# Rotary partner rows moved by transfers, and sample index products in quarter arrays, in a two-layer hybrid decoder step

## The reference

```python
h = rms_norm(x, norm_g) * (1 + scale) + shift
zq, zk, zv, zqi, zki, zwi, ... = split_in(h @ w_in)
q  = rope(rms_norm(zq,  q_norm_g), pos)       # 8 heads of 128
k  = rope(rms_norm(zk,  k_norm_g), pos)       # 2 heads of 128
qi = rope(zqi, pos)                           # 16 index heads of 64
ki = rope(rms_norm(zki, idx_k_norm_g), pos)   # 1 index key of 64

def rope(x, pos):      # rd = width // 4, half = rd // 2
    out = concat([x1 * cos - x2 * sin, x2 * cos + x1 * sin, x[rd:]])

dots  = einsum('bthd,bsd->bths', qi, ki) * 64 ** -0.5
score = einsum('bths,bth->bts', relu(dots), wi)     # then the top k, then attention
```

## Time and profile before

| what | value |
|---|---|
| median of three executions | 3576.96 us |
| the profiled execution: its time, its span | 3580.12 us, 3578.3 us |
| PE busy (matmuls) | 3489.2 us, 98% of the span |
| PEld, DVE, POOL, ACT busy | 3230.0, 1745.4, 1215.5, 1061.9 us |
| granted TensorE clock, mean | 0.99 |
| time of the DMA queue's packets | 53.8% of 16 engines' span |

### The profile page before, as it was taken

How to read it: one execution, slowest core, us unless ns; L and a number is a source line. 1 busy time by engine, 2 the same in 40 slices (tenths; PEclk the granted TensorE clock), 3 DMA queues, 4 the chain that set the end, 5 groups by cost and what they waited for, 6 DMA issues and landing times. The chain is left out here.

```text
span 3578.3 us, 66830 instructions
## 1 busy us (share of the span) xinstructions
PE 3489.2 (98%) x27774; PEld 3230.0 (90%) x27774; DVE 1745.4 (49%) x2484; ACT 1061.9 (30%) x1500; POOL 1215.5 (34%) x508
## 2 busy tenths in 40 slices
PE   5899999999999999999998999999999999999999
PEld 3699988989989989998888999888899998899999
DVE  1413578968987113321115145789689851233201
ACT  2322222222552333222223222222235423332221
POOL 0233333435424223333323333234263232234433
PEclk9799999999999999999999999999999999999999
DMA  9733333656544774658885555444332257644442
GB/s 323 258 104 103 97 104 99 182 171 180 173 126 137 251 229 164 214 192 286 284 283 161 163 156 169 134 127 108 89 111 90 74 174 235 214 157 131 129 122 94
DMA packets 557130, 590.48 MB, mean 165 GB/s; under 512 B 73564, under 2 KB 523377, under 8 KB 546747
## 3 DMA queue, kind: packets, MB, share of 16 engines
q1 hardware_dynamic: 556828, 586.21, 53.8%
HBM read 546.37 MB, written 116.39 MB: 185 GB/s over the span
## 5 line engine op out<-in xcount | busy, mean ns | idle before, releaser
L804 POOL TENSOR_TENSOR w_lo_t<-raw,w_hi_t 128x1024 fp32r<-128x1024 f32 x472 | 1170.5, 2480 | 2339.5 <-ACT w_hi_t L817 2339.5
L1115 PE MATMUL acc<-act_hi,w_hi_t 128*128 128x272 f32 x6528 | 1403.7, 296 | 35.1 <-DVE u_s L1619 14.3
L1115 PE MATMUL acc<-act_hi,w_lo_t 128*128 128x272 f32 x6528 | 1354.0, 289 | 0.0
L1115 PE MATMUL acc<-act_lo,w_hi_t 128*128 128x272 f32 x6528 | 1350.6, 288 | 0.0
L1115 PEld LDWEIGHTS acc<-act_hi,w_hi_t 128*128 128x128 f32 x6528 | 1030.2, 189 | 121.0 <-issue 86.3
L1115 PEld LDWEIGHTS acc<-act_lo,w_hi_t 128*128 128x128 f32 x6528 | 1028.9, 189 | 0.0
L1115 PEld LDWEIGHTS acc<-act_hi,w_lo_t 128*128 128x128 f32 x6528 | 1024.0, 190 | 0.0
L817 ACT ACTIVATE w_hi_t<-raw 128x1024 fp32r<-128x1024 f32 x472 | 499.9, 1059 | 1638.5 <-PE acc L1115 1622.5
L1657 DVE SCALAR_TENSOR_TENSOR conv<-conv,cw 128x512 f32<-128x512 f32 x240 | 197.9, 825 | 70.1 <-POOL w_lo_t L804 70.1
L1115 PE MATMUL acc<-m_hi,w_hi_t 128*128 128x272 f32 x1024 | 215.8, 292 | 0.0
L1115 PE MATMUL acc<-m_hi,w_lo_t 128*128 128x272 f32 x1024 | 211.5, 288 | 0.0
(11 more groups left out here) (242 smaller groups left out, 2714.2 us busy)
## 6 DMA issues: line engine op xcount, KB each, us to landing
raw<-in_w_in_dram SPq DMA_DIRECT2D x272, 512.0 KB, 3.7
ada_ring<-in_w_ada_dram SPq DMA_DIRECT2D x95, 512.0 KB, 7.2
raw<-in_w_in_dram SPq DMA_DIRECT2D x136, 256.0 KB, 3.3
k_near<-in_cache_k_dram SPq DMA_DIRECT2D x256, 128.0 KB, 2.8
v_near<-in_cache_v_dram SPq DMA_DIRECT2D x256, 128.0 KB, 2.7
k_ring<-k_near SPq DMA_DIRECT2D x64, 512.0 KB, 5.1
v_page<-v_near SPq DMA_DIRECT2D x64, 512.0 KB, 6.5
raw<-in_w_out_dram SPq DMA_DIRECT2D x64, 512.0 KB, 4.2
```

What stands on the lines that cost most here:

```text
L804: pool.tensor_tensor(w_lo_t[:, m % 2], raw[:, m % 4], w_hi_t[:, m % 2].bitcast(F32), ALU.subtract).then_inc(S.w_lo, 1)
L1115: last = pe.matmul(acc[:, 2 * m + h, 0:HALF], w[:, c % 2, k, P * m:P * m + P], r[:, kt, h * HALF:(h + 1) * HALF], start=first and k == 0 a ...
```

## The change

1. `tile_extras` no longer makes the exchanged rows. SP, in its `aside`, waits until ACT has evicted the tile and copies the partner rows from `stage[:, m]` to `stage[:, 6 + m]` by transfers within SBUF (`swap_rows`): four of 8 rows x 544 columns for tiles of index heads, two of 16 rows for K and Q. DVE clears `stage[:, 6:8]` once a layer, behind `layer_input`, since the other rows have to be zero. `rope` waits for the transfers (`swap_in`), multiplies the tile by the cosine and the exchanged rows by the sine, both in SBUF, and goes on as before. Index query tiles have no PE work left behind their halves.
2. `dots_s` runs once per sequence: four products of 64 x 64 x 512 (rows 64 p, output partitions 64 c with c = (f + p) mod 2), bank p of `aux`. One relu of 2 x 512 columns follows, and one mixing piece of four products of 64 x 32 x 512 in step 3. `qi_blk` has 64 columns and is not cleared any more. The wait for `conv_s_done` moves from the first product to `dots_tail`, and `turn_kx` waits for the relu of the sequence before.
3. Some semaphores are merged or renamed (`q_blocked`, `blanks_set`, `v_taken`), with the numbers that are waited for.

```diff
+def swaps(g):
+    if g == N_V:
+        return []
+    if g < N_K:
+        return [(a + 8 * s, a + 8 - 8 * s, 8) for a in (0, ID) for s in range(2)]
+    return [(16 * s, 16 - 16 * s, 16) for s in range(2)]
...
+            def swap_rows(l, g, m):
+                if g == N_KI and m == 1 or g == N_V:
+                    return
+                sp.wait_ge(acc_free[m], acc_set(l, g) + 1)
+                if g == N_KI or g == N_QI and m == 1:
+                    sp.wait_ge(S.blanks_set, 3 + l)
+                for to, at_, rows_ in swaps(g):
+                    sp.dma_start(stage[to:to + rows_, 6 + m, :], stage[at_:at_ + rows_, m, :]).then_inc(swap_in[m], 16)
...
                 if l > 0 and 1 <= n < 17:
                     gather([(x, kv) for x in staged_at(n, i)], S.kv_staged)
+                if 1 <= n <= N_GLU and i < 2:
+                    swap_rows(l, n - 1, i)
...
-                    elif s <= 2:
-                        f = 17 * l + 2 * b + s
-                        act.wait_ge(S.sdots_ready, f)
-                        if 2 * b + s > 2:
-                            act.wait_ge(S.mixed, f - 2)
-                        act.activation(relu_s[:, s - 1, :], aux[:, 2, :], ACT.Relu).then_inc(S.srelu_done, 1)
+                    elif s == 1:
+                        act.wait_ge(S.sdots_ready, 9 * l + b + 1)
+                        if b >= 1:
+                            act.wait_ge(S.mixed, 9 * l + b)
+                        act.activation(relu_s[:, :, :], aux[:, 0:2, :], ACT.Relu).then_inc(S.srelu_done, 1)
...
-                    if g == N_KI or g >= N_K:
-                        j = 0 if g == N_KI else 1 + m if g == N_K else 3 + 2 * (g - N_Q) + m
-                        need(pe, S.std_ready, 11 * l + j)
-                        fp32_pair(0, con[:, T_ONE64:T_ONE64 + P] if g == N_KI else ones, stage[:, 2 + m, :])
-                    sw = T_SWI if g < N_K else T_SWQ
-                    last = fp32_pair(2, con[:, sw:sw + P], stage[:, m, :])
+                    j = 0 if g == N_KI else 1 + m if g == N_K else 3 + 2 * (g - N_Q) + m
+                    need(pe, S.std_ready, 11 * l + j)
+                    last = fp32_pair(0, con[:, T_ONE64:T_ONE64 + P] if g == N_KI else ones, stage[:, 2 + m, :])
...
-                need(pe, S.kx_copied, 8 * l + b)
+                need(pe, S.srelu_done, 9 * l + b)
...
-                pe.matmul(aux[:, 2, :], qi_blk[:, b, :], kx_t[:, f, :], start=True, stop=True).then_inc(S.sdots_ready, 1)
+                for f in range(2):
+                    for p in range(2):
+                        c = (f + p) % 2
+                        last = pe.matmul(aux[64 * c:64 * c + 64, p, :], qi_blk[64 * p:64 * p + 64, b, :], kx_t[64 * p:64 * p + 64, f, :],
+                                         start=True, stop=True)
+                last.then_inc(S.sdots_ready, 1)
...
-                for p in range(2):
-                    j = 2 * f + p
-                    last = pe.matmul(aux[32 * j:32 * j + 32, 3, :], mixw[:, p, b, :], relu_s[:, f, :], start=b == 0, stop=b == SEQS - 1)
+                for f in range(2):
+                    for p in range(2):
+                        c, j = (f + p) % 2, 2 * f + p
+                        last = pe.matmul(aux[32 * j:32 * j + 32, 3, :], mixw[64 * c:64 * c + 64, c, b, :], relu_s[64 * c:64 * c + 64, p, :],
+                                         start=b == 0, stop=b == SEQS - 1)
...
-                    if 1 <= s <= 2:
-                        dots_s(l, b, s - 1)
-                    if s >= 2:
-                        mix_s(l, b, s - 2)
+                    if s == 1:
+                        dots_s(l, b)
+                    if s == 3:
+                        mix_s(l, b)
...
-                dve.tensor_tensor(pair(swapped), aux[:, 2:4, 0:HALF], pair(cs[:, sin, :]), ALU.mult).then_inc(S.swap_used, 1)
+                dve.wait_ge(swap_in[m], swap_landed(l, g, m))
                 st.then(dve.tensor_tensor(x, x, cs[:, cos, :], ALU.mult))
+                st.then(dve.tensor_tensor(swapped, swapped, cs[:, sin, :], ALU.mult))
```

More of the change, by code:

```diff
@@ L284, in values_at, with swap_landed @@
     return logits_at(b) + 3
+def swaps(g):
[4 more added lines that the diff above has]
+    return [(16 * s, 16 - 16 * s, 16) for s in range(2)]
+def swap_landed(l, g, m):
+    tiles = [x for x in range(N_GLU) if not (x == N_KI and m == 1)]
+    return 16 * sum(len(swaps(x)) * (l + (x <= g)) for x in tiles)
 def staged_at(n, i):
@@ L372, in trunk_kernel @@
         relu_p = at(C + 7808, "relu_p", [P, 2, 512])
-        qi_blk = at(C + 9408, "qi_blk", [P, SEQS, P])
+        qi_blk = at(C + 9408, "qi_blk", [P, SEQS, 64])
         kx = at(C + 11072, "kx", [P, 2, 2, 4, 2, ID])
@@ L1156, in tile_extras @@
             def tile_extras(l, g, m):
-                if g == N_KI and m == 1:
+                if g == N_KI and m == 1 or N_QI <= g < N_K:
                     return
-                r = 0 if g == N_KI else 2 * g - 1 + m
                 if g == N_KI and l == 1:
@@ L1247, in mix_s @@
                 last.then_inc(S.mixed, 1)
             def dots_tail(l):
-                pe.wait_ge(S.srelu_done, 17 * l + 16)
+                pe.wait_ge(S.srelu_done, 9 * l + 8)
+                pe.wait_ge(S.conv_s_done, 8 * l + 8)
                 for b in range(SEQS):
-                    last = pe.matmul(aux[0:64, 2, STEPS * b:STEPS * b + STEPS], qi_blk[0:64, b, 0:64],
+                    last = pe.matmul(aux[0:64, 2, STEPS * b:STEPS * b + STEPS], qi_blk[0:64, b, :],
                                      ki_new[0:64, SEQ + STEPS * b:SEQ + STEPS * b + STEPS], start=True, stop=True)
@@ L1551, in rope @@
                 r = 0 if g == N_KI else 2 * g - 1 + m
[L1552 removed]
                 if g == N_V:
+                    dve.wait_ge(S.aux_ready, 13 * l + 4 + m)
                     dve.tensor_copy(v_tok[:, 0:4, m * HD:(m + 1) * HD], aux[:, 2, :].rearrange("p (t d) -> p t d", t=4)).then_inc(S.rope_done, 1)
[L1555 removed]
+                    dve.tensor_copy(v_tok[0:NS, 4, m * HD:(m + 1) * HD], aux[0:NS, 3, 0:P]).then_inc(S.v_taken, 1)
                     return
@@ L1572, in rope @@
                     st.wait()
-                    dve.tensor_tensor(out, swapped, std, ALU.mult).then_inc(S.rope_done, 1)
+                    dve.tensor_tensor(out, x, std, ALU.mult).then_inc(S.rope_done, 1)
                 else:
-                    dve.tensor_tensor(out, swapped, x, ALU.add).then_inc(S.rope_done, 1)
+                    dve.tensor_tensor(out, x, swapped, ALU.add).then_inc(S.rope_done, 1)
             def tok(l):
@@ L1663, in turn_qi @@
                 dve.wait_ge(S.tok_stored, 96 * (l + 1))
-                st.then(dve.memset(qi_blk[:, :, :], 0.0))
-                st.wait()
                 dve.wait_ge(S.rope_done, 21 * l + 21)
@@ L1669, in turn_qi @@
                         src = qi[64 * h:64 * h + 64, :, SEQ:TOK].rearrange("p j (b t) -> p b j t", t=STEPS)
-                        c0 = 64 * p + 32 * h
-                        last = dve.tensor_copy(qi_blk[64 * p:64 * p + 64, :, c0:c0 + 32].rearrange("p b (j t) -> p b j t", t=STEPS), src)
-                last.then_inc(S.diag_done, 1)
+                        last = dve.tensor_copy(qi_blk[64 * p:64 * p + 64, :, 32 * h:32 * h + 32].rearrange("p b (j t) -> p b j t", t=STEPS), src)
+                last.then_inc(S.q_blocked, 1)
             def as_bias(work, scores):
@@ L1742, in turn_q @@
                     last = dve.tensor_copy(q_blk[:, :, g, 16 * g:16 * g + 16].rearrange("p b (j t) -> p b j t", t=STEPS), src)
-                last.then_inc(S.qblk_done, 1)
+                last.then_inc(S.q_blocked, 1)
             def keep_k(l, b, j):
@@ L2028, in _ @@
                 layer_input(l)
+                dve.memset(stage[:, 6:8, :], 0.0).then_inc(S.blanks_set, 1)
                 for n in range(NG):
```

51 lines of the change are left out of this document (23 added, 28 removed).

## The result

The kernel after takes 3520.42 us (median of four executions, 3518.45 to 3521.8) against 3578.5 us for the kernel before on the same chip (3575.09 to 3582.82). The ratio is 0.9838, with a 95% interval of 0.9822 to 0.9853. The profiled execution has a span of 3519.5 us, 58.8 us under the one before. The forecast was 3517.0 us: 60.0 us less than before, where the medians now differ by 58.1 and the spans by 58.8.

The account below looks back on a forecast made before the run. PE was taken as the bound between its waits at the places touched. 34.8 + 26.2 - 1.0 = 60.0 us off the median 3576.96 gave 3517.0 us, with 3509 to 3536 for 8 in 10.

Parts of the forecast that it names:

- Exchange products removed: Rotary tiles: 38 tiles each lose exchange products costing 0.915 us, taking 34.8 us off PE.
- Index products: Samples' index products: a sequence's pieces fall from 4.08 to 2.44 us (dots 1.26, mixing 1.18), 26.2 us over 16.
- What waits in the index stage: Index stage: DVE's 35.1 us of waiting for POOL cover rounds that shrink by 0.82 us, so nothing is charged.
- New transfers: Partner-row transfers: tight only at the last rotary tile, 0.3 us left there; charged 0.5 us a layer, 1.0 us.
- three signs that I had named for being wrong: PE's idle time growing over 3 us, a four-product piece over 1.6 us, or transfers landing later than 5 us.
- Rival A: Mixing products of two row groups take turns at bank 3 of `aux`: 3544.5 us, or 3530.8 with two turns; chance 0.13.
- B: Transfers land late, so `rope` holds the key transposes or ACT's eviction, and PE: 3522 us at 6 us landings; chance 0.10.
- C: Index stage's quarter products run one after another, 7.60 us a sequence, and the kernel gets slower: 3599.5 us; chance 0.02.
- D: ACT and POOL set the rotary stage's pace, so the 34.8 us return as waits for `w_lo`: 3551 us; chance 0.02.

Follow-up runs that it names:

- swaps_later: The change with the transfers of the partner rows issued one chunk (6.0 us) later for every tile; span 3540.5 us.
- two_quarters: The change with the four dots products put into two quarters of the array, leaving out half of the samples' scores; span 3529.3 us.
- gate_later: The change with DVE's wait for POOL in the convolution steps put one chunk later in the index stage; 3520.38 us (0.9843).
- after_again: The changed kernel run once more, unedited; 3521.57 us, span 3519.8 us.
- index_only: The kernel before with item 2 of the change only (quarter products, one relu, one mixing piece a sequence); 3552.31 us (0.9932).
- joined: The change with the mixing piece of each sequence placed directly behind the dots of the next; 3521.18 us (0.984).
- rows_grouped: The change with the four products of each index piece reordered so that those reading the same rows are neighbours; span 3517.1 us.

## Why the prediction was right, by its own steps

- *Exchange products removed*, 34.8 us: 34.84 measured, at the places that were named.
- *Index products*, 26.2 us: the dots cost 1.22 us, not 1.26, and the mixing 1.18 as taken. That is 2.40 a sequence and 16 x 1.68 = 26.9 us off PE. Both costs were taken from rows of before, one of row groups and one of column groups, and both carried over to quarters.
- *What waits in the index stage*: this step failed. It said that DVE's 35.1 us of waiting for POOL cover rounds that are 0.82 us shorter. DVE's idle time was not what mattered. What mattered was that its wait is the pause in which POOL can finish. When DVE is a round behind, it passes the wait at once and runs its taps without a pause. The longest POOL step had 8.05 us before and PE a wait of 0.41 behind it; at 9.09 it is 2.14. That is 2.2 us in layer 0 and 3.4 in layer 1, 5.6 us against a stage without taps; but the kernel before paid part of that too, so that it cost the forecast 3.3 of its 26.9.
- *New transfers*, 1.0 us: nothing. The transposes of the keys start at 430.37 without a wait, and `rope` of the last tile ends at 429.70, so 0.67 us are left where I had 0.3, and the charge of 1.0 was not due. Its last product takes 0.72 us there (0.93 in the mean of its kind), not the 1.56 of the earlier trace rows. The 32 waits of DVE for these transfers, 301.8 us, stand in the place of 345.5 for PE and cost nothing. The six us that I had left for ACT's evictions elsewhere were too many at one place: the keys' second tile is done at 306.03 us and ACT evicts V at 308.89, 2.9 us later. That is why swaps_later, with its transfers 6 us later, made PE wait there.
- The sum: 34.84 + 23.56 = 58.4 of 58.8 us; the other stages add up to 0.4. The misses of 2.6 and 1.0 us have opposite signs, so the total came out closer than its terms, and that is luck. The forecast lies 3.4 us under the median; 1.5 of these are the median of before, which rose from 3576.96 to 3578.5 us with the fourth execution.
- Of the three signs that I had named for being wrong, one came true: PE's idle time grew by 3.6 us, more than 3. The waits for POOL account for 4.1 us of it (4.6 to 8.7), 3.4 of them those of the step that failed.
- Rival A is refuted: four mixing products of two row groups into one bank cost 1.18 us, and 1.18 with neighbours exchanged; two turns would be 2.0. The rule that the Trainium skill states in TensorEngine Tiling (Array Packing), Gotcha 1: PSUM Pressure (two row tiles do not access one bank at the same time, and software must see to it) did not cost anything here, where the two write different partitions. B did not occur, though swaps_later shows what it would cost: 8.6 us for a wait of 4.7. C is refuted by the cost of the pieces, 1.22 and 1.18 for four products each; in two_quarters those of one quarter did take turns. D did not occur.

## What to carry to other kernels

When an edit shortens a stretch of the bound engine, divide that stretch's new round by what the helpers need together, not each alone: DVE and POOL here need 7.5 to 7.7 us one after the other, and a round of 7.65 leaves next to no room, although each engine taken alone is far from busy all the time. A wait that is taken away may have been hiding the next one, so mend both or count neither (gate_later alone gained nothing; with the consumer half a chunk later the two index stages took 5.6 us less). A short wait of PE can cost twice its length, when the granted clock falls behind it. Four products in four quarters of the array cost 1.22 us here where one full product costs 0.86, in both orders that were run.

## What the runs showed of the hardware

- A wait of PE of 4.7 us was followed by a granted clock of 0.50 for some 10 us, so that it cost 8.6. Short waits differ from execution to execution. The clock stayed at 1.00 behind the wait of 2.14 us in the change (692 to 696 us), and was 0.50 for 3.4 us, at a cost of some 1.5 us, behind the same wait in layer 1 of after_again, index_only, joined and rows_grouped. It was 0.50 behind the 1.8 us of gate_later in both layers.
- A POOL step of 2.40 us took 9.09 beside DVE taps that read two operands from SBUF and followed each other without a pause, and in turn single taps took 2.87 in place of 0.74 us where they met POOL.
- An SBUF to SBUF transfer of 8 or 16 rows took 0.57 to 1.15 us to issue on SP (median 0.62), the first two-operand step of DVE starting 2.65 us behind the issue of a pair (420.71 to 423.36).
